# Attention: two query blocks of a stream multiplied with the values at once

## The chip, the cores and the metric

The kernel runs on 1 core of one Trainium2 chip. The metric is the device time of one execution in microseconds (us). Below, PE is TensorE (its matmuls), PEld its weight loads, ACT is ScalarE, DVE is VectorE, POOL is GpSimd, SP the engine whose queue issues the weight transfers.

## What is computed

Two layers of a transformer-like block over 256 latent tokens and 256 context tokens, all in float32. In each layer one input projection feeds an attention, two convolution branches and gates; then follow an output projection and a feed-forward part. The change is in the attention alone:

```
def attend(q_nope, q_rope, k_nope, k_rope, v):
    scale = (QK_NOPE + QK_ROPE) ** -0.5
    s = jnp.einsum('bqhd,bkhd->bhqk', q_nope, k_nope) + jnp.einsum('bqhr,bkr->bhqk', q_rope, k_rope)
    p = jax.nn.softmax(s.astype(jnp.float32) * scale, axis=-1).astype(v.dtype)
    return jnp.einsum('bqhk,bkhd->bqhd', p, v)
...
        att_c = attend(qc_nope, qc_rope, kc_nope, kc_rope, vc)
...
        att = blockwise_attend(q_nope, q_rope,
                               jnp.concatenate([k_nope, kc_nope], axis=1),
                               jnp.concatenate([k_rope, kc_rope], axis=1),
                               jnp.concatenate([v, vc], axis=1))
```

There are 8 heads, 64 value columns each. Latent queries see 512 keys (latent and context), context queries see 256 (context alone). The context stream is needed in layer 0 only.

## The kernel before

Every engine runs a program of its own, in an order that is written out by hand, and they meet at semaphores. The order of PE's work is that of the code of its block; no scheduler changes it.

The attention goes over four pairs of heads (pairs 0 to 3), and in a pair over the query blocks that `duos_of(l)` lists, 128 queries each: in layer 0 two latent blocks with four key tiles (`kt` = 4) and two context blocks with two (`kt` = 2), in layer 1 the two latent blocks. Block d of a pair goes through these steps, for both heads h of the pair:

- PE `scores(d, h)` (L2570): one product into the PSUM bank `scores` h, up to 512 columns wide.
- DVE `soften(d)`: the largest score (L1700); ACT `exps(d)`: the exponentials and their sum (L991); DVE: reciprocal (L1704) and the probabilities `PR` (L1706), which sets `prob_done`.
- PE `turn(d, h)` (L2579): `kt` transposes of 128 columns into the one PSUM bank `PT` ("probsT"); it waits for `prob_done` and for ACT's copy of the turn before it.
- ACT `copies(d)` (L1001): PSUM to SBUF, into `PTs`, one buffer for each head; it sets `turned_copied`.
- PE `attend(p, d)` (L2593): for each key tile and head one product, 64 weight columns (the values of a head) and 128 moving columns (turned probabilities of the block), accumulated in `attended` (`PV`). The two heads write to partitions 0 to 63 and 64 to 127. It waits for the copies of both heads, and sets `pv_done`.

In `pair(p)`, PE's order for each block but the last is: turn(d, 0), scores(d+1) for both heads, turn(d, 1), some other work, attend(d). The other work fills PE while ACT and DVE make the next block's probabilities: parts of a gate's projection (`gate_parts`, L2550 to L2552), or the next pair's keys and queries (`keys_tile`, `query_tile`, L2081 to L2083). For the last block it is turn(d, 0), gate work, turn(d, 1), gate work, attend(d), the rest of the gate. In the fp32 products the trace has two PE instructions for one of the program; the transposes have one.

ACT's order between two blocks matters too. After `copies(d)` and `exps(d+1)` it does, at one place of each pair, the gate's tanh (L966) and the rounding of a weight tile (`look`, L402), and before the last block's copies `keys_out` (L952, two instructions) and, for some pairs after the first of these copies, for others ahead of both, `queries_out` (L958, L960):

```
                    for d in range(len(duos) - 1):
                        copies(d)
                        exps(d + 1)
                        if d == NS[l] - 1:
                            gate_out(gate_a, p * 2)
                            look(next(looks))
                    if not last:
                        ...
                        keys_out(following[0])
                        if len(following) == 2:
                            copies(len(duos) - 1, [0])
                        queries_out(following[1])
```

`len(following) == 2` holds for pairs 0 and 2; pair 3 (`last`) has none of this.

Of the kernel before, what the change touches and what calls it, by code (L numbers as in the profile page):

```python
# [8 lines left out]
SEQ = 256  # L9
# [156 lines left out]
def build(nc, x, c, ctx_in, c_ctx, w_mod, b_mod, ln1_g, w_in, q_a_norm_g, w_q_b, kv_a_norm_g,  # L166
# [6 lines left out]
    with stack:  # L173
        def sb(name, shape, dt=F32):
            return stack.enter_context(nc.sbuf_tensor(name, shape, dt))
# [19 lines left out]
        ATT = sb("ATT", [P, 7 * T])  # L195
        Qb = ATT[:, 0:2 * T].rearrange("p (h n) -> p h n", h=2)
        Kb = ATT[:, 2 * T:4 * T].rearrange("p (h n) -> p h n", h=2)
        PTs = ATT[:, 4 * T:6 * T].rearrange("p (h n) -> p h n", h=2)
        ROW = ATT[:, 6 * T:7 * T]
        PR = sb("PR", [P, 2, T])  # L200
        KR = PR[NOPE:NOPE + ROPE, 0, :]
# [11 lines left out]
        RT = sb("RT", [P, 4])  # L213
        LINES = sb("LINES", [P, 2, D])
        GATE_ROW, GAIN_ROW = LINES[:, 0, :], LINES[:, 1, :]
        RSTD = sb("RSTD", [P, T])
        Z = sb("Z", [P, 2, T])
        TAB = sb("TAB", [P, 2, T])
# [212 lines left out]
        def duos_of(l):  # L431

            return [(s * SEQ + q * P, 2 * s, 4 - 2 * s) for s in range(NS[l]) for q in range(2)]
# [6 lines left out]
        def _(sp):  # L440
# [60 lines left out]
            for l in range(DEPTH):  # L501
# [51 lines left out]
                if l:  # L553
                    sp.dma_start(GAIN_ROW, final_g.partition_broadcast(P)).then_inc(rows_in, 16)
                if l == 0:
                    sp.wait_ge(pv_done, len(duos_of(0)) * PAIRS)
                sent = 0

                def loaded():
# [221 lines left out]
        def _(act):  # L781
# [101 lines left out]
            for l in range(DEPTH):  # L883
# [95 lines left out]
                def pair(p):  # L979

                    last, looks = p == PAIRS - 1, iter(pair_looks(p))
                    at.ring = 0

                    def exps(d):

                        kt = duos[d][2]
                        for h in range(2):
                            act.wait_ge(max_done, at.unit.n + (2 * d + h + 1))
                            if d:
                                act.wait_ge(turned, at.unit.n + (2 * d + h - 1))  # L990
                            act.activation(PR[:, h, 0:kt * P], S[h][:, 0:kt * P], ACT.Exp, bias=NM[:, h:h + 1],  # L991
                                           accum_out=RS[:, h:h + 1]).then_inc(exp_done, 1)

                    def copies(d, heads=range(2)):

                        kt = duos[d][2]
                        for h in heads:
                            act.wait_ge(turned, at.unit.n + (2 * d + h + 1))
                            if d:
                                act.wait_ge(pv_done, at.duo.n + d)  # L1000
                            act.activation(PTs[:, h, 0:kt * P], PT[:, 0:kt * P], ACT.Copy).then_inc(turned_copied, 1)  # L1001

                    exps(0)
                    look(next(looks))
                    gate_a = at.tile()
# [7 lines that stand above are left out]
                        following = [at.tile() for _ in range(3 if queries_kind(p + 1) == "fours" else 2)]  # L1013
# [4 lines that stand above are left out]
                    copies(len(duos) - 1, [1] if not last and len(following) == 2 else range(2))  # L1018
                    if not last:
                        look(next(looks))  # L1020
                        look(next(looks))
                    gate_b = at.tile()
                    act.wait_ge(pv_done, at.duo.n + len(duos))
                    act.activation(Uhi[:, p + AT0, 0:TQ], PV[:, 0:TQ], ACT.Copy).then_inc(op_hi, 1)
                    at.operand.next()
                    gate_out(gate_b, p * 2 + 1)
                    at.unit.n += 2 * len(duos)
                    at.duo.n += len(duos)

                for p in range(PAIRS):  # L1030
                    pair(p)
# [1022 lines left out]
        def _(pe):  # L2054
# [414 lines left out]
            for l in range(DEPTH):  # L2469
# [111 lines left out]

                def attend(p, d):

                    col, k0, kt = duos[d]
                    if d == 0 and p:
                        pe.wait_ge(op_lo, at.operand.n)
                    if d == 0 and p == 0:
                        for t in vt:
                            pe.wait_ge(drained[t.bank], t.drained)
                    pe.wait_ge(turned_copied, at.unit.n + 2 * d + 2)  # L2590
                    for k in range(kt):
                        for h in range(2):
                            last = pe.matmul(PV[h * VH:(h + 1) * VH, col:col + P],  # L2593
                                             V[:, k0 + k, (2 * p + h) * VH:(2 * p + h + 1) * VH],
                                             PTs[:, h, k * P:(k + 1) * P], start=k == 0, stop=k == kt - 1)
                    last.then_inc(pv_done, 1)

                for p in range(PAIRS):
# [11 lines left out]
                    for d in range(len(duos) - 1):  # L2610
# [8 lines left out]
                        else:  # L2619
# [5 lines left out]
                                nopes = query_tile(slot, 0)  # L2625
                            if fours and (d == 2 or l == 1):
                                query_tile(slot, 1)
                        attend(p, d)
                    d = len(duos) - 1
                    turn(d, 0)  # L2630
                    next(gate_b)
# [196 lines left out]
```

## Time and profile before

| | |
|---|---|
| time, median of 3 runs | 1222.69 us (1222.45 to 1223.12) |
| the profiled execution's own time | 1222.99 us |
| its span in the profile | 1221.2 us |
| busy: PE, DVE, ACT, POOL | 98%, 71%, 43%, 16% of the span |
| mean granted TensorE clock | 0.999 of full speed |

The attention of layer 0 lies at about 140 to 245 us of the span, that of layer 1 at about 864 to 928 us. A row of the timeline gives start, length, engine, line, operation, tiles, shapes, a count (several instructions of one kind are merged: the length then runs from the first one's start to the last one's end), and in brackets the engine's idle time before it with what ended it. PE's lengths overlap, since a matmul starts before the one ahead of it has left the array; what PE spends is therefore read from start to start.

### The profile page before, as it was taken

Reading aid. Unit: us, or ns where it says so; the run is one execution under the profiler, and the core shown is the slowest. Engines: PE = TensorE matmul, PEld = TensorE weight load, DVE = VectorE, ACT = ScalarE, POOL = GpSimd, SP = SyncE. Lnnn points to the kernel's source line nnn. Section 1 sums busy time; section 2 is a strip of 40 time slices with the busy share of each in tenths; the row PEclk is TensorE's granted clock in tenths of the full one; section 3 lists DMA queues with packets and bytes.
Section 4 is the critical chain, followed back from the end, with each engine's and each line's share of the span. In section 5 each row is a group of like instructions: output and inputs, shape, how many; then the busy total and the mean of one; then the engine's idle time right before and its main releaser. Section 6 shows DMA issues by size and latency. Waiting matters only on the chain.

```text
span 1221.2 us, 17807 instructions
## 1 busy us (share of the span) xinstructions
PE 1199.4 (98%) x6834; PEld 997.7 (82%) x6834; DVE 866.6 (71%) x1286; ACT 530.0 (43%) x891; POOL 191.9 (16%) x158
## 2 busy tenths in 40 slices
PE   7999999999999999999999999999999999999997
PEld 5777777788888898888888888889879999888886
DVE  4675766586887487678765666699887877766666
ACT  4342565522534352222222223465664555655554
POOL 0106993000001200000000000302980002000000
PEclk9999999999999999999999999999999999999999
DMA  9956322134464436557664665335434674666662
GB/s 296 315 153 206 84 54 69 36 86 132 110 178 131 156 105 191 152 163 217 187 193 153 209 192 157 101 90 149 122 114 113 168 212 138 201 196 190 181 198 87
DMA packets 265252, 188.88 MB, mean 155 GB/s; under 512 B 16035, under 2 KB 250833, under 8 KB 265169
## 3 DMA queue, kind: packets, MB, share of 16 engines
q1 hardware_dynamic: 264832, 187.60, 52.7%
q8 instruction: 55, 0.90, 0.3%
q14 instruction: 28, 0.23, 0.1%
q10 hardware_dynamic: 337, 0.15, 0.0%
HBM read 186.67 MB, written 1.05 MB: 154 GB/s over the span
## 4 chain that ended last, share of the span: by engine, by line
PE 89%; DVE 3%; ACT 3%; SPq 2%; issue 2%; DMA 1%; ACTq 0%; DVEq 0%
PE bank L2081 18%; PE bank L2083 17%; PE bank L2082 17%; PE bank L2122 5%; PE bank L2120 3%; PE scores L2570 3%; PE bank L2550 2%; PE bank L2552 2%; PE bank L2551 2%; PE probsT L2579 2%; PE attended L2593 1%; SPq L494 1%; ACT Whi L402 1%; DVE Wlo L413 1%; PE bank L2649 1%
## 5 line engine op out<-in xcount | busy, mean ns | idle before, releaser
L413 DVE TENSOR_TENSOR Wlo<-Wraw,Whi 128x1024 fp32r<-128x1024 f32 (+3 forms) x294 | 323.3, 1108 | 104.2 <-ACT Whi L402 103.1
L402 ACT ACTIVATE Whi<-Wraw 128x1024 fp32r<-128x1024 f32 (+1 forms) x296 | 270.4, 928 | 125.6 <-PE bank L2083 72.0
L2081 PE MATMUL bank<-Hhi,Whi 128*128 128x512 f32 (+1 forms) x786 | 285.6, 363 | 1.7 <-DVE Wlo L413 1.4
L2082 PE MATMUL bank<-Hlo,Whi 128*128 128x512 f32 (+1 forms) x786 | 281.6, 358 | 0.0
L2083 PE MATMUL bank<-Hhi,Wlo 128*128 128x512 f32 (+1 forms) x786 | 281.5, 358 | 0.0
L2081 PEld LDWEIGHTS bank<-Hhi,Whi 128*128 128x128 f32 x786 | 148.4, 189 | 30.6 <-issue 6.6
L2082 PEld LDWEIGHTS bank<-Hlo,Whi 128*128 128x128 f32 x786 | 148.5, 189 | 22.2 <-issue 1.0
L2083 PEld LDWEIGHTS bank<-Hhi,Wlo 128*128 128x128 f32 x786 | 148.5, 189 | 22.0
L2081 PE MATMUL bank<-Uhi,Whi 128*128 128x512 f32 (+1 forms) x350 | 128.3, 367 | 0.2 <-issue 0.2
L2083 PE MATMUL bank<-Uhi,Wlo 128*128 128x512 f32 (+1 forms) x350 | 126.5, 362 | 0.0
L2082 PE MATMUL bank<-Ulo,Whi 128*128 128x512 f32 (+1 forms) x350 | 126.5, 361 | 0.0
L670 POOL TENSOR_TENSOR SUM<-SUM,V 128x512 f32<-128x512 f32 (+1 forms) x21 | 28.4, 1354 | 486.9 <-ACT V L801 486.7
L2122 PE MATMUL bank<-Hhi,Whi 128*128 128x512 f32 x287 | 102.3, 396 | 0.0
L724 POOL TENSOR_SCALAR SUM<-U,PAR 128x512 f32<-128x512 f32 (+1 forms) x56 | 81.1, 1448 | 53.7 <-DVE ACC L1603 48.4
L2120 PE MATMUL bank<-Hhi,Wlo 128*128 128x256 f32 x328 | 84.7, 279 | 0.0
L2081 PEld LDWEIGHTS bank<-Uhi,Whi 128*128 128x128 f32 x350 | 66.0, 189 | 11.7 <-issue 2.1
L2083 PEld LDWEIGHTS bank<-Uhi,Wlo 128*128 128x128 f32 x350 | 66.0, 189 | 10.2
L2082 PEld LDWEIGHTS bank<-Ulo,Whi 128*128 128x128 f32 x350 | 66.1, 189 | 10.0 <-issue 0.2
L1848 DVE SCALAR_TENSOR_TENSOR X<-bank,MOD,X 128x256 f32<-128x256 f32 x64 | 28.1, 478 | 55.3 <-PE bank L2083 52.9
L791 ACT ACTIVATE V<-bank 128x512 f32<-128x512 f32 (+1 forms) x48 | 24.4, 508 | 94.7 <-PE bank L2083 94.7
L727 POOL TENSOR_TENSOR ACC<-ACC,SUM 128x512 f32<-128x512 f32 (+1 forms) x56 | 64.7, 1155 | 4.7
L1352 DVE SCALAR_TENSOR_TENSOR G<-ATT,CV,G 128x1024 f32<-128x1024 f32 x50 | 64.7, 1319 | 0.0
(309 smaller groups left out, 1977.6 us busy)
## 6 DMA issues: line engine op xcount, KB each, us to landing
Wraw<-in_w_ff SPq DMA_DIRECT2D x126, 512.0 KB, 3.9
Wraw<-in_w_in SPq DMA_DIRECT2D x78, 512.0 KB, 4.0
ATT<-in_w_mod SPq DMA_DIRECT2D x58, 512.0 KB, 4.5
Wraw<-in_w_o SPq DMA_DIRECT2D x16, 512.0 KB, 4.1
ACC<-in_w_mod SPq DMA_DIRECT2D x14, 512.0 KB, 4.4
Wraw<-in_w_mla_o SPq DMA_DIRECT2D x8, 512.0 KB, 3.5
ATT<-in_w_mod SPq DMA_DIRECT2D x12, 256.0 KB, 8.4
Wraw<-in_w_kv_b SPq DMA_DIRECT2D x12, 256.0 KB, 4.1
```

The costliest lines, as they stand in the source:

```text
L402: last = act.activation(hi, raw, ACT.Copy)
L413: last = eng.tensor_tensor(lo, raw, hi.bitcast(F32), ALU.subtract)
L670: pool.tensor_tensor(SUM[:, 0:n], SUM[:, 0:n], SQ[:, slot, 0:n], ALU.add).then_inc(sq_summed, 1)
L724: v = mark(pool.tensor_scalar(by_stream(SUM[:, :], l), U[:, 1, 0:NS[l], w:w + SEQ], PAR[:, l, CDW + 2 * w + 1:CDW + 2 * w + 2], None, ALU. ...
L727: ins = pool.tensor_tensor(by_stream(ACC[:, 1, :], l), by_stream(ACC[:, 1, :], l), by_stream(SUM[:, :], l), ALU.add)
L1352: last = dve.scalar_tensor_tensor(acc(s), raw, c, acc(s), mult, add)
L2081: pe.matmul(dst, sh, mh, start=j == 0, stop=False)
L2082: pe.matmul(dst, sh, ml, start=False, stop=False)
L2083: last = pe.matmul(dst, sl, mh, start=False, stop=j == k - 1)
L2120: last = pe.matmul(banks[t.bank][:, half[0]], Wlo[:, slot, w], Hhi[:, j, half[0]], start=False, stop=False)
L2122: last = pe.matmul(banks[t.bank][:, :], Whi[:, slot, w], Hhi[:, j, :], start=False, stop=j == DT - 1)
L2570: pe.matmul(S[h][:, 0:kt * P], Qb[0:NOPE + ROPE, h, col:col + P], Kb[0:NOPE + ROPE, h, k0 * P:(k0 + kt) * P], start=True, stop=True).then_ ...
```

## The change

`attend` is no longer called for every block but for every second one (odd d). It multiplies the turned probabilities of both blocks of a stream with the values at once: the same 64 weight columns, 256 moving columns. For this `PTs` holds both blocks: head 0's lie where both heads' buffers were (`ATT`), head 1's in `GATE_ROW` (`LINES`), which is used later, in layer 1, for something else. ACT's copy writes the `kt` tiles of 128 columns 256 columns apart instead of side by side. The waits on `pv_done` count half as many steps.

```
-        PTs = ATT[:, 4 * T:6 * T].rearrange("p (h n) -> p h n", h=2)
...
+        PTs = [w.rearrange("p (k n) -> p k n", k=4) for w in (ATT[:, 4 * T:6 * T], GATE_ROW)]
...
-                    sp.wait_ge(pv_done, len(duos_of(0)) * PAIRS)
+                    sp.wait_ge(pv_done, len(duos_of(0)) // 2 * PAIRS)
...
-                            if d:
-                                act.wait_ge(pv_done, at.duo.n + d)
-                            act.activation(PTs[:, h, 0:kt * P], PT[:, 0:kt * P], ACT.Copy).then_inc(turned_copied, 1)
+                            if d >= 2:
+                                act.wait_ge(pv_done, at.duo.n + d // 2)
+                            act.activation(PTs[h][:, 0:kt, d % 2 * P:(d % 2 + 1) * P],
+                                           PT[:, 0:kt * P].rearrange("p (k n) -> p k n", k=kt),
+                                           ACT.Copy).then_inc(turned_copied, 1)
...
-                    col, k0, kt = duos[d]
-                    if d == 0 and p:
+                    col, k0, kt = duos[d - 1]
+                    if d == 1 and p:
...
                     for k in range(kt):
                         for h in range(2):
-                            last = pe.matmul(PV[h * VH:(h + 1) * VH, col:col + P],
+                            last = pe.matmul(PV[h * VH:(h + 1) * VH, col:col + SEQ],
                                              V[:, k0 + k, (2 * p + h) * VH:(2 * p + h + 1) * VH],
-                                             PTs[:, h, k * P:(k + 1) * P], start=k == 0, stop=k == kt - 1)
+                                             PTs[h][:, k, :], start=k == 0, stop=k == kt - 1)
...
-                        attend(p, d)
+                        if d % 2:
+                            attend(p, d)
```

PE's order in layer 0, pair 0, from the end of the work that fills block 0 on, before (scores 128x256 are those of block 2; x8 counts the program's products):

```order
L2552 MATMUL bank<-Hhi,Wlo 128x512
L2593 MATMUL attended<-ATT,V 64x128 x8
L2579 MATMUL probsT<-IDN,PR 128x128 x4
L2570 MATMUL scores<-ATT 128x256 x2
L2579 MATMUL probsT<-IDN,PR 128x128 x4
L2081 MATMUL bank<-Uhi,Whi 128x512
L2082 MATMUL bank<-Ulo,Whi 128x512
L2083 MATMUL bank<-Uhi,Wlo 128x512
L2081 MATMUL bank<-Uhi,Whi 128x512
L2082 MATMUL bank<-Ulo,Whi 128x512
L2083 MATMUL bank<-Uhi,Wlo 128x512
L2593 MATMUL attended<-ATT,V 64x128 x8
```

The same place of the changed kernel, whose lines there are numbered two higher:

```order
L2554 MATMUL bank<-Hhi,Wlo 128x512
L2581 MATMUL probsT<-IDN,PR 128x128 x4
L2572 MATMUL scores<-ATT 128x256 x2
L2581 MATMUL probsT<-IDN,PR 128x128 x4
L2083 MATMUL bank<-Uhi,Whi 128x512
L2084 MATMUL bank<-Ulo,Whi 128x512
L2085 MATMUL bank<-Uhi,Wlo 128x512
L2083 MATMUL bank<-Uhi,Whi 128x512
L2084 MATMUL bank<-Ulo,Whi 128x512
L2085 MATMUL bank<-Uhi,Wlo 128x512
L2595 MATMUL attended<-ATT,V 64x256
L2595 MATMUL attended<-LINES,V 64x256
```

The eight products of block 0 are gone from between the filling work and turn(1, 0); after the next filling work stand eight of 256 columns (two are shown) in the place of eight of 128.

Layer 1, pair 0, from the end of the filling work to the place behind turn(1, 1), before:

```order
L2083 MATMUL bank<-Uhi,Wlo 128x256
L2593 MATMUL attended<-ATT,V 64x128 x8
L2579 MATMUL probsT<-IDN,PR 128x128 x4
L2550 MATMUL bank<-Hhi,Whi 128x256
L2551 MATMUL bank<-Hlo,Whi 128x256
L2552 MATMUL bank<-Hhi,Wlo 128x256
L2550 MATMUL bank<-Hhi,Whi 128x256
L2551 MATMUL bank<-Hlo,Whi 128x256
L2552 MATMUL bank<-Hhi,Wlo 128x256
L2579 MATMUL probsT<-IDN,PR 128x128 x4
L2550 MATMUL bank<-Hhi,Whi 128x256
L2551 MATMUL bank<-Hlo,Whi 128x256
```

And of the changed kernel:

```order
L2085 MATMUL bank<-Uhi,Wlo 128x256
L2581 MATMUL probsT<-IDN,PR 128x128 x4
L2552 MATMUL bank<-Hhi,Whi 128x256
L2553 MATMUL bank<-Hlo,Whi 128x256
L2554 MATMUL bank<-Hhi,Wlo 128x256
L2552 MATMUL bank<-Hhi,Whi 128x256
L2553 MATMUL bank<-Hlo,Whi 128x256
L2554 MATMUL bank<-Hhi,Wlo 128x256
L2581 MATMUL probsT<-IDN,PR 128x128 x4
L2552 MATMUL bank<-Hhi,Whi 128x256
L2553 MATMUL bank<-Hlo,Whi 128x256
L2554 MATMUL bank<-Hhi,Wlo 128x256
```

Here too the eight products ahead of turn(1, 0) are gone. The six products of the gate between turn(1, 0) and turn(1, 1) are the same, and what follows them ends in one `attend` of 256 columns. On ACT no instruction changes its place.

## Rows read from the trace of the kernel before

**Rows 1.** The profile page: part 1 (busy engines) and part 4 (the chain).

```profile
PE 1199.4 (98%) x6834; PEld 997.7 (82%) x6834; DVE 866.6 (71%) x1286; ACT 530.0 (43%) x891; POOL 191.9 (16%) x158
...
PE 89%; DVE 3%; ACT 3%; SPq 2%; issue 2%; DMA 1%; ACTq 0%; DVEq 0%
```

**Rows 2.** Groups of PE instructions by form: the products with the values.

```profile
L2593 PE MATMUL attended<-ATT,V 128*64 128x128 f32 x320 | 22.8, 280 | 0.0
```

**Rows 3.** Timeline of layer 0, pair 0, engine PE (start, length, line).

```profile
145.05 0.39 PE L2552 MATMUL bank<-Hhi,Wlo 128*128 128x512 f32 x1
145.28 0.60 PE L2579 MATMUL probsT<-IDN,PR 128*128 128x128 f32 x4
145.72 1.88 PE L2570 MATMUL scores<-ATT 96*128 96x512 f32 x4
...
150.41 0.39 PE L2552 MATMUL bank<-Hhi,Wlo 128*128 128x512 f32 x1
150.73 1.09 PE L2593 MATMUL attended<-ATT,V 128*64 128x128 f32 x16
...
152.24 1.03 PE L2570 MATMUL scores<-ATT 96*128 96x256 f32 x4
```

**Rows 4.** The same timeline at a query block with two key tiles.

```profile
159.36 0.39 PE L2083 MATMUL bank<-Uhi,Wlo 128*128 128x512 f32 x1
159.68 0.66 PE L2593 MATMUL attended<-ATT,V 128*64 128x128 f32 x8
```

**Rows 5.** Timeline of PE at 256-column products in column groups, outside the attention.

```profile
374.90 1.07 PE L2364 MATMUL scores<-ATT,ROWSEL 128*32 128x256 f32 x16
```

**Rows 6.** Timeline of DVE in layer 0, pair 0: normalised probabilities.

```profile
149.58 0.49 DVE L1706 TENSOR_SCALAR PR<-PR,RR 128x512 f32<-128x512 f32 x1
...
159.22 0.35 DVE L1706 TENSOR_SCALAR PR<-PR,RR 128x256 f32<-128x256 f32 x1
```

**Rows 7.** Timeline of PE in layer 1, pair 0.

```profile
875.06 0.66 PE L2579 MATMUL probsT<-IDN,PR 128*128 128x128 f32 x4
876.67 0.63 PE L2579 MATMUL probsT<-IDN,PR 128*128 128x128 f32 x4 [0.24 <-ACT ATT L1001]
```

**Rows 8.** Timeline of ACT and DVE in the same stretch.

```profile
871.67 0.60 ACT L1001 ACTIVATE ATT<-probsT 128x512 f32<-128x512 f32 x1 [1.56 <-PE probsT L2579]
...
873.76 1.07 ACT L402 ACTIVATE Whi<-Wraw 128x1024 fp32r<-128x1024 f32 x1
874.71 1.19 ACT L952 ACTIVATE ATT<-bank 64x512 f32<-64x512 f32 x2
875.92 0.60 ACT L1001 ACTIVATE ATT<-probsT 128x512 f32<-128x512 f32 x1
...
873.17 0.49 DVE L1706 TENSOR_SCALAR PR<-PR,RR 128x512 f32<-128x512 f32 x1
```

**Rows 9.** Timeline of ACT in layer 1, pairs 1 and 3.

```profile
892.60 0.38 ACT L960 ACTIVATE ATT<-bank 64x256 f32<-64x256 f32 x1
893.11 0.60 ACT L1001 ACTIVATE ATT<-probsT 128x512 f32<-128x512 f32 x1
...
923.47 1.07 ACT L402 ACTIVATE Whi<-Wraw 128x1024 fp32r<-128x1024 f32 x1
924.42 0.61 ACT L1001 ACTIVATE ATT<-probsT 128x512 f32<-128x512 f32 x1
```

**Rows 10.** Timeline of ACT and PE in layer 0, pair 1, last block.

```profile
189.03 0.60 ACT L960 ACTIVATE ATT<-bank 64x512 f32<-64x512 f32 x1
189.65 0.39 ACT L1001 ACTIVATE ATT<-probsT 128x256 f32<-128x256 f32 x1
...
190.23 0.39 PE L2579 MATMUL probsT<-IDN,PR 128*128 128x128 f32 x2
```

**Rows 11.** Timeline of PE and its loads in layer 0, pair 3.

```profile
238.02 0.41 PE L2579 MATMUL probsT<-IDN,PR 128*128 128x128 f32 x2 [0.36 <-ACT ATT L1001]
...
240.43 0.20 PEld L2579 LDWEIGHTS probsT<-IDN,PR 128*128 128x128 f32 x2 [0.26 <-DVE PR L1706]
```

More of the change, by code:

```diff
@@ L1022, in pair @@
                     gate_b = at.tile()
-                    act.wait_ge(pv_done, at.duo.n + len(duos))
+                    act.wait_ge(pv_done, at.duo.n + len(duos) // 2)
                     act.activation(Uhi[:, p + AT0, 0:TQ], PV[:, 0:TQ], ACT.Copy).then_inc(op_hi, 1)
@@ L1027, in pair @@
                     at.unit.n += 2 * len(duos)
-                    at.duo.n += len(duos)
+                    at.duo.n += len(duos) // 2
                 for p in range(PAIRS):
@@ L2582, in attend @@
                 def attend(p, d):
-                    col, k0, kt = duos[d]
-                    if d == 0 and p:
+                    col, k0, kt = duos[d - 1]
+                    if d == 1 and p:
                         pe.wait_ge(op_lo, at.operand.n)
-                    if d == 0 and p == 0:
+                    if d == 1 and p == 0:
                         for t in vt:
```

## The prediction

> **What bounds the kernel now.** I read the page first. PE is busy for 98% of the span and holds 89% of the chain that ended last, while DVE and ACT are far from full [rows 1]. So time is what PE spends from instruction to instruction, plus the few places where it waits. The second view is the groups of PE by form: the products with the values are 320 PE instructions (160 of the program) that keep PE busy for 22.8 us in all [rows 2], under 2% of the span. The change can only move some of that, and what stands around it. The third view is the timeline of PE, and there I read gaps from start to start. The fourth is the timeline of ACT and DVE at the same places, to see how long before PE's arrival a block's probabilities and copies were ready. That decides whether work taken away from PE makes it earlier or makes it wait.
>
> **The change part by part.** The number of weight loads and instructions is halved; the columns that stream are as many as before.
>
> One `attend` with four key tiles, in its place. With it, from the last product of the filling work to the scores behind the next turn, PE takes 152.24 - 150.41 = 1.83 us; at a place without one, the same stretch takes 145.72 - 145.05 = 0.67 us [rows 3]. So it costs 1.16 us. The 16 instructions last 1.09 us and the 8 of a block with two key tiles 0.66 us [rows 3, 4]: four steps, each with two instructions started together (one of each head), are 0.43 us, so a step is 0.108 us. The streaming of eight steps is then 0.86 us and the rest, 1.16 - 0.86 = 0.30 us, is paid once for each `attend`: going into products of 64 weight columns and out again. With two key tiles it is 1.16 - 0.43 = 0.73 us in its place.
>
> A step with 256 columns is not in the trace for these products. Bounds: below, twice 0.108 = 0.216 us. Above, (1.07 - 0.38) / 3 = 0.23 us from the 16 instructions of 256 columns that go in four column groups at once, four steps with the last instruction's 0.38 us taken off [rows 5]; that mean holds a longer first step, as every group has. I take 0.216. Widening an `attend` then adds 8 x 0.108 = +0.87 us with four key tiles and +0.43 with two. At 0.23 it would be +0.98 and +0.49, in all 0.9 + 0.2 = 1.1 us more.
>
> The Trainium skill, TensorEngine Tiling, section Tiling Modes, says that changing the tiling mode drains TensorE, while changing the tile within a mode doesn't. By that rule the 0.30 us are the two changes of mode around each `attend`, and the trace agrees with a loss of that kind; by that rule alone, each change of mode saved would be time saved, which is the first rival.
>
> Where the removed `attend` frees PE, PE goes straight on to turn(d+1, 0). Twelve are removed: eight in layer 0, four in layer 1. If nothing waits, each merge saves 1.16 - 0.87 or 0.73 - 0.43, both about -0.30 us. So each place has to be looked at.
>
> Layer 0, first merge of a pair (blocks 0 and 1), four times. Pair 0's probabilities of block 1 are ready at 149.58 + 0.49 = 150.07, and PE would come at 150.41 + 0.23 = 150.64 (0.23 us from a gate's last product to a turn, 145.05 to 145.28) [rows 3, 6]. 0.57 us to spare, and what follows (the copy, the turn of head 1) hangs on that turn alone. -0.29 each.
>
> Layer 0, second merge (blocks 2 and 3). In pairs 0 and 2 the probabilities of block 3 were ready at 159.22 + 0.35 = 159.57 and PE would have come at 159.36 + 0.23 = 159.59 [rows 4, 6]. That is no margin, but the work of ACT and DVE ahead of them moves 1.16 us earlier against PE, since it now falls beside the longer `attend` of block 1. -0.30 each, -0.59 a pair.
>
> Pair 1 is different: ACT does both instructions of `queries_out` ahead of the copy of turn(3, 0). It starts that copy at 189.65, right behind L960, and is done at 190.04; turn(3, 1) stood at 190.23 [rows 10]. With the usual 0.15 us from a copy's end to the turn behind it (875.92 + 0.60 to 876.67 [rows 7, 8]) it could come 0.04 us earlier and no more. The 0.73 us taken from PE there become a wait, and the widened `attend` adds 0.43. Pair 1: -0.29 - 0.04 + 0.43 = +0.10.
>
> Pair 3 has short filling work. PE waits 0.36 us for a copy at turn(2, 1) and then for the probabilities at turn(3, 0), 240.43 [rows 11]. The first wait goes away, since the longer `attend` of block 1 covers it; the second stays, but ACT's and DVE's chain up to it is 1.16 us earlier. So turn(3, 0) is 1.16 earlier, 0.06 more is saved behind it (a turn of four transposes lasts 0.66 us with an `attend` ahead of it and 0.60 without [rows 3, 7]), and +0.43 comes back: -0.79.
>
> Layer 0 in all: -0.59 - 0.59 + 0.10 - 0.79 = -1.87 us.
>
> Layer 1 is where the cost lies. In pair 0 ACT is busy without a gap from the copy at 871.67 on: copy, exponentials, gate, weight tile at 873.76, `keys_out` at 874.71, and only at 875.92 the copy of turn(1, 0), done at 876.52. Turn(1, 1) stands at 876.67 and had waited for it [rows 7, 8]. Turn(1, 0) itself at 875.06 could be 1.16 us earlier: its probabilities are ready at 873.17 + 0.49 = 873.66 [rows 8]. But turn(1, 1) can't, because nothing on ACT has moved. Thus the `attend` of block 0 lay in time in which PE would otherwise have waited. Taken away it gives nothing; put behind turn(1, 1), onto the path, it costs the whole +0.87 us. Pair 2 repeats this (no queries ahead of the copy). In pair 3 the copy at 924.42 follows the weight tile's start at 923.47 by 0.95 us [rows 9], the same 0.95 as from 873.76 to 874.71 [rows 8]: ACT is the limit there too. In pair 1 ACT ends `queries_out` at 892.60 + 0.38 = 892.98 and copies at 893.11 [rows 9], so 0.11 us can be had. Layer 1: 3 x 0.87 + 0.76 = +3.37 us.
>
> The same page of the skill, section Performance Considerations, warns that tiling speeds up TensorE but not the emptying of PSUM. Here the trace agrees in layer 1: the copy out of `probsT` is what turn(1, 1) waits for.
>
> The copies themselves: 48 of 0.60 or 0.39 us, now written 256 columns apart. The trace has no such write; the rows of copies from `probsT` side by side [rows 8, 10] are all there is. I take no change. Cover: in layer 1 there is none, three copies of a pair are on the path. No step is added on SP, POOL or DVE, and no transfer. SP's wait on `pv_done` ends at the same instruction of PE.
>
> Sum: -1.87 + 3.37 = +1.5 us. The profiled execution's own time is 1222.99, 0.3 above the median of 1222.69, and its span 1221.2. From 1222.99 it is 1224.5; against the median, **1224.2 us**.
>
> **The rivals.** (1) *Every merge pays.* Only the streaming and the 0.30 us of each `attend` count, and layer 1 doesn't wait for ACT. 12 x -0.29 = -3.5: 1219.2 us. It is decided by one thing: whether ACT can start the copy of turn(1, 0) in layer 1 as early as PE would then be done with it, 1.1 us ahead of 875.92. For: probabilities are ready in time nearly everywhere. Against: ACT's unbroken row up to 875.92 [rows 8]. This is where the Trainium skill's page TensorEngine Tiling, Tiling Modes, read alone, would lead.
>
> (2) *The spaced copy is slower.* Three copies a pair in layer 1 and one or two in layer 0 are on the path, some 18. From 0.06 us more for each, the kernel is slower by over 0.2%; at 0.1 it is +1.8: 1226.0.
>
> (3) *The two heads no longer run together at 256 columns.* A step becomes 0.43 us: 8 x 8 x 0.216 + 4 x 4 x 0.216 = +17 us, 1241. Against it: the 256-column products in column groups, 16 in 1.07 us [rows 5].
>
> (4) *The loss in layer 1 is partly absorbed*, by ACT reaching the copies sooner in two of the pairs: about 1222.7 to 1223.3.
>
> **How the numbers follow.** Forecast 0.65, its own range 1223.3 to 1225.6 (bounds of the step above, a few tenths for pairs 1 and 3). Rival 1 0.09, rival 2 0.12, rival 3 0.04, rival 4 0.10. 0.2% is 2.4 us, about what a measurement of this kernel can tell from no change: under 1220.3 is faster, over 1225.1 slower. Faster: 0.09. Slower: rivals 2 and 3, and the top of the forecast, 0.19. Same: 0.72. Range 1221.5 to 1226.1: it leaves out rival 1, rival 3 and the worse half of rival 2, about 0.18.
>
> **What would show it.** Right: `attended` in 160 PE instructions with starts in pairs 0.216 us apart; PE at turn(1, 0) of layer 1 1.1 us earlier than before within its pair and at turn(1, 1) not, with PE's wait for ACT's copy there grown from 0.24 [rows 7] to about 1.4 us in three pairs; the stretch of layer 1's attention 3.4 us longer, that of layer 0 1.9 shorter. Wrong: copies of L1001 longer than 0.60 and 0.39 us; a stretch of layer 1 that isn't longer; or a wait elsewhere, above all for DVE ahead of turn(3, 0) in layer 0.

## The result, and the profile after

The changed kernel takes **1226.45 us** (median of 11 runs, 1225.07 to 1227.15); the kernel before, run beside it 11 times, 1223.1. The ratio is **1.0026, 95% interval 1.0018 to 1.0034**: slower by 3.3 us, where 1.5 were forecast. The profiled execution took 1226.33 us, its span is 1224.4.

The page of the changed kernel (parts 1 and 4; before: [rows 1]):

```profile
PE 1197.0 (98%) x6674; PEld 993.8 (81%) x6674; DVE 867.4 (71%) x1286; ACT 531.2 (43%) x891; POOL 193.7 (16%) x158
...
PE 84%; DVE 4%; ACT 4%; DMA 2%; issue 2%; ACTq 0%; SPq 0%; DVEq 0%
```

PE has 160 instructions fewer and 2.4 us less busy time, and the kernel is slower. So the time lost is time in which PE waits: it isn't busy for 1224.4 - 1197.0 = 27.4 us, before 1221.2 - 1199.4 = 21.8. PE's share of the chain fell from 89% to 84%, which is far more than 3 us; it shows that the chain runs through waits for other engines more often, not how much they cost. The groups by form say that the operations themselves cost what was assumed (busy, mean ns; before: [rows 2, 8, 10]):

```profile
L2595 PE MATMUL attended<-LINES,V 128*64 128x256 f32 x80 | 19.8, 387 | 0.0
L2595 PE MATMUL attended<-ATT,V 128*64 128x256 f32 x80 | 19.7, 385 | 0.4
...
L1001 ACT ACTIVATE ATT<-probsT 128x512 f32<-128x512 f32 x16 | 9.6, 598 | 11.5 <-PE probsT L2581 11.4
```

The two halves of `attended` run beside each other, so 39.5 us of busy time are not 39.5 us of span. The copies that write 256 columns apart (head 0's are shown) take 598 ns, as long as those side by side (0.60 us in [rows 8]).

The timeline of the changed kernel, all that the text below reads (start, length, engine, line; in brackets the idle time before and what ended it):

```profile
140.62 0.59 PE L2572 MATMUL scores<-ATT 96*128 96x512 f32 x1
...
154.03 0.38 PE L2595 MATMUL attended<-ATT,V 128*64 128x256 f32 x1
...
155.33 0.38 PE L2595 MATMUL attended<-ATT,V 128*64 128x256 f32 x1
...
174.78 1.29 POOL L727 TENSOR_TENSOR ACC<-ACC,SUM 128x512 f32<-128x512 f32 x1
175.03 1.32 DVE L1708 TENSOR_SCALAR PR<-PR,RR 128x512 f32<-128x512 f32 x1
176.41 0.66 PE L2581 MATMUL probsT<-IDN,PR 128*128 128x128 f32 x4 [0.17 <-DVE PR L1708]
...
188.91 0.39 ACT L1001 ACTIVATE ATT<-probsT 128x256 f32<-128x256 f32 x1
189.44 0.41 PE L2581 MATMUL probsT<-IDN,PR 128*128 128x128 f32 x2 [0.53 <-ACT ATT L1001]
...
243.49 0.39 PE L2652 MATMUL bank<-Uhi,Whi 128*128 128x512 f32 x1
...
862.59 1.02 PE L2572 MATMUL scores<-ATT 96*128 96x512 f32 x2
...
872.26 0.60 PE L2581 MATMUL probsT<-IDN,PR 128*128 128x128 f32 x4
873.02 1.19 ACT L952 ACTIVATE ATT<-bank 64x512 f32<-64x512 f32 x2
874.23 0.60 ACT L1001 ACTIVATE ATT<-probsT 128x512 f32<-128x512 f32 x1
874.98 0.63 PE L2581 MATMUL probsT<-IDN,PR 128*128 128x128 f32 x4 [1.41 <-ACT ATT L1001]
875.64 0.60 ACT L1001 ACTIVATE LINES<-probsT 128x512 f32<-128x512 f32 x1
876.38 0.40 PE L2595 MATMUL attended<-ATT,V 128*64 128x256 f32 x1
...
929.47 0.39 PE L2652 MATMUL bank<-Uhi,Whi 128*128 128x256 f32 x1
...
1002.26 1.06 ACT L402 ACTIVATE Whi<-Wraw 128x1024 fp32r<-128x1024 f32 x1 [0.86 <-DMA Wraw<-in_w_o]
...
1004.64 0.39 PE L2312 MATMUL bank<-Uhi,Whi 128*128 128x256 f32 x1 [0.84 <-DVE Wlo L413]
```

The rows of the kernel before that answer to some of them and were not shown yet:

```profile
140.82 0.59 PE L2570 MATMUL scores<-ATT 96*128 96x512 f32 x1
...
174.96 1.30 POOL L727 TENSOR_TENSOR ACC<-ACC,SUM 128x512 f32<-128x512 f32 x1
175.83 0.71 DVE L1706 TENSOR_SCALAR PR<-PR,RR 128x512 f32<-128x512 f32 x1
...
245.19 0.39 PE L2649 MATMUL bank<-Uhi,Whi 128*128 128x512 f32 x1
...
864.28 1.02 PE L2570 MATMUL scores<-ATT 96*128 96x512 f32 x2
...
877.33 0.60 ACT L1001 ACTIVATE ATT<-probsT 128x512 f32<-128x512 f32 x1
877.98 1.09 PE L2593 MATMUL attended<-ATT,V 128*64 128x128 f32 x16
...
927.52 0.38 PE L2649 MATMUL bank<-Uhi,Whi 128*128 128x256 f32 x1
```

The first and the last product of a stage cut the span into pieces: the first scores of a layer's attention (L2572, before L2570) and the first output product behind it (L2652, before L2649). Layer 0 is 243.49 - 140.62 = 102.87 us, before 245.19 - 140.82 = 104.37; layer 1 is 66.88 us, before 63.24; behind it lie 1224.40 - 929.47 = 294.93 us, before 1221.21 - 927.52 = 293.69. So layer 0 gave 1.50 us, layer 1 cost 3.64, and **1.24 us were lost where nothing was changed**. With the start (-0.20) and the stretch between the layers (+0.01) that is the 3.19 us between the spans. All runs were cut in the same way. In the last two columns w_o is layer 1's first transfer of `in_w_o` behind the attention, and the load is explained at its experiment.

```
                          start   layer 0  (its pair 1)  layer 1   behind   load, us from first w_o issue
before                    140.8   104.37   28.32         63.24     293.69    +0.7
after                     140.6   102.87   28.77         66.88     294.93    +3.9
e1_again                  141.9   102.90   28.77         66.87     294.50    +3.8
e2_layer0_only            141.6   102.87   28.77         63.22     293.74    -3.3, +11.5
e3_layer1_only            140.7   104.50   28.36         66.88     293.75    -6.8,  +9.7
e4_moved_not_widened      140.5   103.00   28.82         66.96     293.75    +0.6
e5_early_waits            140.6   102.89   28.79         66.56     295.19    +3.7
e6_fewer_pool_taps        141.0   102.47   28.37         66.88     294.75    +3.6
e7_merged_copies_first    140.2   102.87   28.77         63.95     294.62    +4.0
e8_single_copies_first    140.6   104.49   28.35         64.21     293.74    +0.7
f1_load_moved_off         144.4   102.87   28.77         66.89     293.75    -1.8, +13.8
f2_load_moved_on          146.1   104.50   28.35         66.89     294.41    +3.6
f3_layer0_copy_first      140.4   102.17   28.06         63.22     293.75    -3.6, +11.9
f4_both_copies_and_waits  141.3   102.17   28.07         63.61     294.46    +3.6
```

The stages repeat within some 0.05 us from run to run, except the start, which moves by over a microsecond, and the stretch behind in the programs that are slow there. So one profile settles a few tenths of a stage, which the medians can't. For every program but f1 and f2, what the two layers and the stretch behind differ by adds up to within 0.5 us of the difference of the times (medians, where there are several executions).

### The profile page after: what moved, and what is told of

Read it like the earlier page. It is cut to its first block, busy times and chain, and to the rows that moved or that the text cites. A ratio compares the mean times of both kernels' runs of the same rounds, so it can differ in the third digit from the quotient of the medians.

```text
span 1224.4 us, 17471 instructions
## 1 busy us (share of the span) xinstructions
PE 1197.0 (98%) x6674; PEld 993.8 (81%) x6674; DVE 867.4 (71%) x1286; ACT 531.2 (43%) x891; POOL 193.7 (16%) x158
## 4 chain that ended last, share of the span: by engine, by line
PE 84%; DVE 4%; ACT 4%; DMA 2%; issue 2%; ACTq 0%; SPq 0%; DVEq 0%
PE bank L2083 17%; PE bank L2084 17%; PE bank L2085 16%; PE bank L2124 5%; PE bank L2122 3%; PE scores L2572 3%; PE bank L2552 2%; DMA Wraw<-in_w_in 2%; ACT Whi L402 2%; DVE Wlo L413 2%; PE bank L2554 2%; PE bank L2553 2%; PE attended L2595 1%; PE probsT L2581 1%; PE bank L2652 1%
## 5 line engine op out<-in xcount | busy, mean ns | idle before, releaser
L2085 PEld LDWEIGHTS bank<-Hhi,Wlo 128*128 128x128 f32 x786 | 148.5, 189 | 22.1
L724 POOL TENSOR_SCALAR SUM<-U,PAR 128x512 f32<-128x512 f32 (+1 forms) x56 | 84.6, 1510 | 53.7 <-DVE ACC L1605 48.4
L2085 PEld LDWEIGHTS bank<-Uhi,Wlo 128*128 128x128 f32 x350 | 66.0, 189 | 10.3
L2122 PEld LDWEIGHTS bank<-Hhi,Wlo 128*128 128x128 f32 x328 | 61.8, 188 | 3.5
```

The lines of the kernel that those rows point to most:

```text
L724: v = mark(pool.tensor_scalar(by_stream(SUM[:, :], l), U[:, 1, 0:NS[l], w:w + SEQ], PAR[:, l, CDW + 2 * w + 1:CDW + 2 * w + 2], None, ALU. ...
L2085: last = pe.matmul(dst, sl, mh, start=False, stop=j == k - 1)
L2122: last = pe.matmul(banks[t.bank][:, half[0]], Wlo[:, slot, w], Hhi[:, j, half[0]], start=False, stop=False)
```

## The experiments

**The changed kernel once more; each layer alone; the place without the width.** The products of a block are taken at their old place or both blocks' at the new one; `e4` has the new place and 128-column products, block d-1 and then block d. The buffers are the spaced ones in all of them. In this and the later cuts of code, conditions on a run's settings are written out.

```
+MODES = ['merged', 'single']     # e2; e3: ['single', 'merged']; e4: ['moved', 'moved']
...
+for b in {"single": [d], "moved": [d - 1, d], "merged": [d - 1]}[MODES[l]]:
+    col, k0, kt = duos[b]
+    c = slice(0, SEQ) if MODES[l] == "merged" else slice(b % 2 * P, (b % 2 + 1) * P)
...
-if d % 2:
+if d % 2 or MODES[l] == "single":
     attend(p, d)
```

> The changed kernel once more. In its first profile 2.15 us of the 3.3 lost lie in the two attentions (-1.5 in layer 0, +3.65 in layer 1) and 1.2 us behind them, in waits for weight transfers (0.2 us at about 980, 1.0 us at about 1004 us). Theory A: the part behind the attention is chance of one execution, so the two waits are not both there again and the difference to before is 2.0 to 2.6 us. Theory B: a later PE in layer 1 meets the transfers worse each time: both waits are there again and the difference is 3.2 to 3.6 us.

> Merged products in layer 0 alone; in layer 1 each query block has its products of 128 columns in their old place. Both theories: the attention of layer 0 is 1.5 us shorter and that of layer 1 as before (63.2 us from its first scores to the first product of the output), so 1221.6 us, 1.5 faster than before. If the spaced copies cost something, layer 1 is longer than before here too.

> Merged products in layer 1 alone. The attention of layer 1 is 3.6 us longer. Theory A: +3.6 us, 1226.7. Theory B: +4.8 us, 1227.9, with the waits for transfers behind the attention as in the changed kernel's first profile.

> The products of both blocks stay apart, 128 columns each, but stand together where the merged ones stand, in both layers. If the place alone decides, as I think, this is the changed kernel's time within 0.5 us (the same streaming, one entry into 64-column products saved just the same): 1225.3 to 1226.9. If the 256 columns themselves cost or save something (weight loads, the overlap of the two heads), it differs from the changed kernel by more, at 16 more loads for each pair.

Measured: e1 1225.58 us (ratio 1.0021, 1.0012 to 1.0031), e2 1221.08 (0.9986, 0.9977 to 0.9995), e3 1226.55 (1.0029, 1.0018 to 1.0040), e4 1225.21 (1.0018, 1.0009 to 1.0027). The stages add: layer 0 gives 1.5 us with layer 1 as it was, layer 1 loses 3.6 with layer 0 as it was. In e4 the attentions take 103.00 and 66.96 us, the changed kernel's within 0.13: **it is the place that costs and pays, not the width**. Sixteen 128-column products behind turn(1, 1) take what eight of 256 columns take there. The spaced copies alone cost 104.50 - 104.37 = 0.13 us in e3's layer 0 and nothing in e2's layer 1 (63.22 against 63.24). And e2, e3 and e4 lack the loss behind the attention that e1 has again. Neither theory of e1 holds as written. Its median is 2.55 us above the kernel before, as theory A has it, but the loss behind the attention isn't chance: it is back with 0.81 us. Of the two waits of theory B only the later one is back, 0.6 us instead of 0.8.

**Layer 1: the order of ScalarE.** In layer 1 the copies of the last block stand ahead of the next pair's `keys_out` and `queries_out`, as far as what they wait for allows; e7 with merged products, e8 with the products one block at a time.

```
+                        if l == 1 and len(following) == 2:
+                            copies(len(duos) - 1, [0])
                         keys_out(following[0])
+                        if l == 1:
+                            copies(len(duos) - 1, [1] if len(following) == 2 else range(2))
                         queries_out(following[1])
...
+                            if last and l == 1:
+                                copies(len(duos) - 1, [0])
                             look(next(looks))
```

> The changed kernel, and in layer 1 ACT copies the turned probabilities of block 1 before it copies keys and queries of the next pair (in pair 3 before it rounds a weight tile). If ACT's order is what makes the merge lose in layer 1, the merge now gets most of it back: pairs 0 to 2 are 0.85 us shorter, pair 3 0.35, the attention of layer 1 63.9 us instead of 66.9, and the whole about 1222.6 us (-2.9 against the changed kernel). If the wait was not ACT's order, at most 0.2 us a pair.

> The same order of ACT in layer 1, with the products of each block in their old place in both layers: what the order is worth without the merge. PE's turn(1, 0) bounds the copy there, so 0.17 us each in pairs 0 and 2, nothing in 1 and 3: layer 1 62.9 us, the whole 1222.6 us. If the order alone gave the 0.85 us of the merged one, it would be 1220.

Measured: e7 1223.43 us (ratio 1.0002, 0.9993 to 1.0011), layer 1 63.95 us: 2.93 less than in the changed kernel, within 0.05 us of what was expected. So ScalarE's order is the cause of 2.93 of the 3.64 us that layer 1 lost. The median was expected at 1222.6 and missed by 0.8, which is about the loss behind the attention. Timeline of e7, the same place as 872.07 to 876.38 above (lines some 5 to 22 higher):

```profile
871.79 0.60 PE L2599 MATMUL probsT<-IDN,PR 128*128 128x128 f32 x4
...
872.56 0.61 ACT L1006 ACTIVATE ATT<-probsT 128x512 f32<-128x512 f32 x1
873.03 1.20 ACT L957 ACTIVATE ATT<-bank 64x512 f32<-64x512 f32 x2
873.31 0.63 PE L2599 MATMUL probsT<-IDN,PR 128*128 128x128 f32 x4 [0.21 <-ACT ATT L1006]
...
874.99 0.40 PE L2617 MATMUL attended<-ATT,V 128*64 128x256 f32 x1 [0.35 <-ACT LINES L1006]
...
921.33 0.66 PE L2599 MATMUL probsT<-IDN,PR 128*128 128x128 f32 x4 [0.66 <-DVE PR L1726]
```

PE's wait of 1.41 us is down to 0.21. From turn(1, 0) to turn(1, 1) it is now 1.52 us, in the changed kernel 874.98 - 872.26 = 2.72. The last row is from pair 3, which is still 0.65 us longer than before the change: there PE comes to turn(1, 0) before DVE has the probabilities ready, and waits 0.66 us for them.

e8 missed: 1223.93 us (1.0010, 1.0001 to 1.0019), layer 1 64.21 us, 1.0 more than before and not 0.3 less. Its timeline shows why:

```profile
874.93 0.66 PE L2599 MATMUL probsT<-IDN,PR 128*128 128x128 f32 x4
...
875.62 0.60 ACT L1006 ACTIVATE ATT<-probsT 128x512 f32<-128x512 f32 x1 [0.93 <-PE probsT L2599]
876.12 1.19 ACT L957 ACTIVATE ATT<-bank 64x512 f32<-64x512 f32 x2
877.33 0.60 ACT L1006 ACTIVATE LINES<-probsT 128x512 f32<-128x512 f32 x1
...
877.98 0.32 PE L2617 MATMUL attended<-ATT,V 128*64 128x128 f32 x1 [0.27 <-ACT LINES L1006]
```

With the `attend` of block 0 ahead of turn(1, 0), PE reaches that turn late. ScalarE, which now has the copy next, stands idle for 0.93 us, does `keys_out` only then, and the second copy comes late behind it. The old order suits the old place of the products, the new order the new one; neither edit is good by itself.

**Layer 1: the waits that moved.** `op_lo` and the output banks' waits stand at block 0's place again, where before had them; the products stay merged. There is one execution.

```
+def ready(p):
+    if p:
+        pe.wait_ge(op_lo, at.operand.n)
+    else:
+        for t in vt:
+            pe.wait_ge(drained[t.bank], t.drained)
...
 if d % 2:
     attend(p, d)
+elif d == 0:
+    ready(p)
```

> The changed kernel, with the two waits that the first attend of a pair has besides the one for the copies (for the previous pair's output, or for the values) placed where block 0's attend stood before, ahead of turn(1, 0), instead of at the merged attend. In the changed kernel's trace the merged attend of layer 1 starts 0.14 us behind the end of the copy that it waits for, before it was 0.05. Theory: the second wait needs an instruction of its own behind the late one. Then each of the four pairs of layer 1 is 0.09 us shorter, 66.9 to 66.5 us in all. If the 0.09 us belong to the spaced copy or to the 256 columns, nothing changes.

Measured: layer 1 66.56 us, 0.32 less, 0.08 for each pair. In the changed kernel the first merged product starts 876.38 - 876.24 = 0.14 us behind the end of the copy that it waits for; before it was 877.98 - 877.93 = 0.05. That the second wait on the same instruction is what takes the time rests on this edit and its size; the wait has no row of its own in these views.

**Layer 0, pair 1: DVE beside GpSimd.** The kernel leaves out 20 of the 28 convolution taps that GpSimd computes in layer 0. There is one execution.

```
-for w in range(TAPS_BEFORE, TAPS):
+for w in list(range(TAPS_BEFORE, TAPS))[20 if l == 0 else 0:]:
```

> The changed kernel, without 20 of the 28 convolution taps that GpSimd computes in layer 0 (they are left out of the result), so that GpSimd is done before the attention. Theory: in pair 1 of layer 0 the probabilities of block 1 came late because DVE's multiplication took 1.32 us beside GpSimd's addition instead of 0.7. Then it takes about 0.5 us here, PE doesn't wait for it, and pair 1 is 0.3 us shorter, 28.77 to 28.4; the wait for ACT's copy at turn(3, 1) stays. If GpSimd is not the reason, pair 1 stays at 28.77.

Measured: pair 1 28.37 us instead of 28.77, the attention's other pairs as they were. DVE's row at the place of 175.03 above:

```profile
175.37 0.49 DVE L1712 TENSOR_SCALAR PR<-PR,RR 128x512 f32<-128x512 f32 x1
```

The same instruction takes 0.49 us with GpSimd idle, 0.71 in the kernel before and 1.32 in the changed one, where it starts 0.25 us behind the start of GpSimd's addition. In the kernel before it started 0.87 us behind it. In both it ends 0.28 us after that addition (176.35 against 176.07, and 176.54 against 176.26), so the 0.8 us by which DVE came earlier were lost again for the greater part.

**Layer 0, pair 1: the order of ScalarE.** Layer 1 as before, layer 0 merged, and there the copy of turn(3, 0) ahead of `queries_out` in pair 1 too. This is the version to which the experiments point.

```
+MODES = ['merged', 'single']
...
 keys_out(following[0])
-if len(following) == 2:
+if l == 0 or len(following) == 2:
     copies(len(duos) - 1, [0])
 queries_out(following[1])
...
+if l == 0:
+    copies(len(duos) - 1, range(2) if last else [1])
```

> Layer 1 as in the kernel before; layer 0 merged, and in its pair 1 ScalarE copies the last turned block ahead of the next queries' copies instead of behind them. If ScalarE's order is what holds the last turned block of pair 1 up: pair 1 falls from 28.8 us to 28.2 to 28.4, layer 0's attention from 102.9 to 102.3 to 102.5, the median to about 1220.6, ratio 0.998. If DVE beside GpSimd holds it up, or if the later queries' copies cost what the earlier copy gives, pair 1 stays at 28.7 to 28.8 and the median at 1221.1.

Measured: **1220.57 us, ratio 0.9981 (0.9972 to 0.9990)**, the fastest version here. Pair 1 takes 28.06 us, 0.71 less, which is more than was expected (28.2 to 28.4). Timeline of f3 at the place of 188.91 to 189.44 above, with the last instruction of `queries_out` (L965) now behind the copy:

```profile
187.50 0.39 ACT L1006 ACTIVATE ATT<-probsT 128x256 f32<-128x256 f32 x1
...
188.38 0.60 ACT L965 ACTIVATE ATT<-bank 64x512 f32<-64x512 f32 x1
188.58 0.38 PE L2599 MATMUL probsT<-IDN,PR 128*128 128x128 f32 x2
```

The wait of 0.53 us in front of turn(3, 1) is gone.

**Both orders and the waits together.** Both layers merged, with the edits of e7, f3 and e5.

> Both layers merged, the last turned blocks copied ahead of the next keys and queries in both layers, and TensorE's waits on V and on the output buffer put back to where the kernel before has them. If the two causes in layer 1 add (the order of ScalarE 2.9 us, the late wait 0.09 us a pair): layer 1's attention 63.6 us, layer 0's 102.4; the stretch behind stays at 294.6 to 295.2 as long as TensorE's instruction load meets the first w_o transfer; median 1222.4 to 1223.0. If the earlier copy has already hidden the late wait: layer 1 stays at 63.95 and the median at 1223.2.

Measured: 1222.0 us (ratio 0.9993, 0.9985 to 1.0002), layer 0 102.17, layer 1 63.61: the three causes add to within 0.05 us. The median is 0.4 us below the expected range, layer 0 0.2 shorter and the stretch behind 0.1 shorter than expected. Even so layer 1 is 0.37 us longer than before the change. Pairs 0 to 2 are 0.05 to 0.08 us shorter, pair 3 0.58 longer, as in e7.

**The stretch behind the attention.** The loss came with the changed program and not by chance: in every program with both layers merged, in none of e2, e3, e4 and e8. All layers' work there is the same instruction for instruction. What differs is how many instructions PE has done by then, and with it where the loads of its instructions fall. The queue q8 has 53 loads of 16 KB over the span in the changed kernel and 55 before, for 2 x 6674 and 2 x 6834 products and weight loads of PE: one for some 250 PE instructions each time, so these are PE's. For the table they were found by narrowing the window of the DMA view until one 16 KB packet was left in it. Seven runs have a load 3.6 to 4.0 us behind the first w_o issue, and those are the seven whose stretch takes 294.4 to 295.2 us; in the seven others it takes 293.69 to 293.75. The same seven also have a load 10.0 to 10.3 us ahead of that issue, which none of the others has, and in them the first w_o issue itself comes late: 64.2 to 64.5 us behind the first output product (994.0 - 929.47), in the others 63.9 (991.4 - 927.52). The DMA view of the changed kernel, 3 to 5 us behind that issue at 994.0:

```profile
q1 hardware_dynamic: 521, 0.26, 48.7%
q8 instruction: 1, 0.02, 5.8%
...
Wraw<-in_w_o SPq DMA_DIRECT2D x2, 512.0 KB, 5.8
```

And of the kernel before, 3 to 5 us behind its issue at 991.4:

```profile
q1 hardware_dynamic: 536, 0.27, 50.0%
...
Wraw<-in_w_o SPq DMA_DIRECT2D x2, 512.0 KB, 4.5
```

Two kernels move the loads without touching the attention or what follows. They move all loads together, and the start grows. Warm-up products at the very start are cut in two, which adds four PE instructions each: 27 of them in the changed kernel (f1), 15 in e3's kernel (f2). The expectations give the load's place as 0.7 to 1.2 us behind the issue; that was counted on the transfers' own zero, which is some 3 us off that of the timeline, and should read 3.6 to 4.0. For e3's kernel f2's expectation has 4.3, where the table has 9.7; its load moved by 6.1 us and not by the 3.4 asked for. That it still came to the place meant was luck; the table has the place where it fell.

```
 for _ in range(n):
-    pe.matmul(S[1][:, 0:P], ONES[:, :], ONES[:, :], start=True, stop=True)
+    halves = 2 if parted[0] else 1
+    parted[0] -= halves - 1
+    for c in range(halves):
+        w = P // halves
+        pe.matmul(S[1][:, c * w:(c + 1) * w], ONES[:, :], ONES[:, 0:w], start=True, stop=True)
```

> The changed kernel with its 27 warm-up products at the very start (128 columns each) cut into 54 of 64 columns: the same columns on TensorE, about 108 more instructions in its stream, and nothing else. TensorE's instructions are loaded in pieces of 256; in all five programs with both layers merged such a load (16 KB) came 0.7 to 1.2 us behind the issue of layer 1's first w_o transfer, and the stretch behind the attention was 0.8 to 1.5 us longer; in the five others it came elsewhere. Theory A (the place of this load costs the time): 108 instructions at some 0.055 us each move the load about 6 us ahead, so the stretch behind the attention falls from 294.5 to 295.2 us to 293.7, the wait of 0.8 us ahead of the gate product of the first w_o operand goes, the issues of the fourth and fifth w_o transfers take 0.37 us again instead of 0.8 to 1.6, and the median is 1.0 us below that of the changed kernel, less what the start may lose: 1224.9 to 1225.9. Theory B (the changed attention itself shifts the transfers against each other): the stretch stays at 294.5 or more and the median at 1225.6 to 1226.5. The attentions keep 102.9 and 66.9 us by both.

> The opposite of the run before: only layer 1 merged (there the stretch behind the attention was 293.75 us, and the load came 4.3 us behind the first w_o issue), with 15 of the warm-up products cut in two, 60 more instructions, which should bring the load to about 0.9 us behind that issue. Theory A: the stretch behind the attention becomes 294.5 to 295.2 us, with slow issues of the fourth and fifth w_o transfers, and the median goes from 1226.5 to about 1227.4. Theory B: it stays at 293.75 and the median at 1226.5.

Measured: with the load moved off, the stretch is 293.75 us although both layers are merged; with it moved on, 294.41 although only layer 1 is. Both go as theory A has it, in opposite directions (f2 0.1 us short of its range). So the place of the loads is the cause. Which of the two, the one 10 us ahead or the one 3.6 to 4.0 us behind, these two kernels can't tell apart, since both come and go together; what speaks for the second is that PE's main wait and the slow fourth and fifth issues lie behind it. The rows on the transfers, first of the changed kernel from 994.0 us on (issues' length in ns, min/median/max; who waited; time to landing):

```profile
L451 SPq DMA_DIRECT2D Wraw<-in_w_o x6: 368/379/1383, 994.0 to 1004.6; - x6
...
  PE bank L2312: 0.8, 1
...
DMA to landing us min/median/max: 4.0/5.7/6.2
```

of f1:

```profile
L455 SPq DMA_DIRECT2D Wraw<-in_w_o x6: 367/373/563, 997.1 to 1007.2; - x6
...
DMA to landing us min/median/max: 3.9/4.9/5.6
```

and of f2:

```profile
L455 SPq DMA_DIRECT2D Wraw<-in_w_o x6: 367/378/910, 1000.9 to 1011.1; - x6
...
  PE bank L2316: 0.4, 1
...
DMA to landing us min/median/max: 3.7/5.5/5.8
```

The issues grow from 0.37 to 1.38 and 0.91 us, the landings are 0.6 to 0.8 us later than in f1, and PE waits. The medians were missed: f1 1231.61 us (1.0077, 1.0059 to 1.0096) and f2 1232.95 (1.0082, 1.0068 to 1.0097). The cut warm-up is not free: 32 instructions of 64 columns last 7.06 us where 16 of 128 columns lasted 3.39, so a half takes the time of a whole. The start grew by 2.5 us (f1 against e1) and more, and f1's single times scatter from 1228.5 to 1237.6. So the medians say nothing on the load; the stage lengths do.

## Why the prediction was wrong

The direction, the mechanism of both layers and the sizes of the parts on PE were right. The time was 2.25 us too low, and the range missed by 0.35 us. By the prediction's own borders (over 1225.1 is slower) the result is "slower", which had 0.19, mostly for rivals 2 and 3, and these fell; "same" had 0.72. Part of the 2.25 isn't the change's: the forecast stood on 1222.69 for the kernel before, and beside the changed kernel that took 1223.1, 0.41 more; counted from there the range would just have held. The step that failed is the one that put everything outside the attention at nothing (1.24 us); two terms in the attention were too small (0.37 and 0.27 us). By its own steps:

- **A step of 0.216 us at 256 columns**: (155.33 - 154.03) / 6 = 0.217 us, over six steps. The upper bound of 0.23 wasn't needed. The third rival, the heads one after the other, fell.
- **-0.30 us for each merge where nothing waits**: pair 0 and pair 2 of layer 0 went from 26.25 us each to 25.66 and 25.64, -0.59 and -0.61; forecast -0.59. Pair 3: -0.74; forecast -0.79. That 0.30 us is paid once for each `attend` rests on e4 too, which saves as much with 128 columns. The Trainium skill, TensorEngine Tiling, Tiling Modes, says that a change of mode drains TensorE; what is saved in layer 0 agrees with it, and by that rule alone layer 1 would have gained as well.
- **Pair 1 of layer 0, +0.10**: it was +0.45. Here a step failed: "0.57 us to spare" was read in pair 0 and used for the first merge of all four pairs. In pair 1 GpSimd's additions run, DVE's normalisation took 1.32 us, and PE waited at turn(1, 0): the profile puts 0.17 us of idle time there, and without most of the taps the pair is 0.40 shorter. In that kernel (e6) pair 1 takes 28.37 us, +0.05, near the forecast. ScalarE's order was named as the limit of the second merge, rightly: undoing it gives 0.71 us (f3).
- **Layer 1, 0.87 and 0.76 for a pair**: measured +0.93, +0.84, +0.93, +0.94. That turn(1, 1) can't move was exact: PE waited 1.41 us there, forecast 1.4. The term left out is the 0.08 us a pair of the waits that moved with the first `attend` (e5) and that the step "The change part by part" gave no price. Without it layer 1 would be +3.32, forecast +3.37. The fourth rival, a loss partly absorbed, fell, and so did the first: it hung on ScalarE starting the copy early, which only an edit of its order brings (e7).
- **Spaced copies, no change**: 598 ns as before. Rival 2 fell.
- **Nothing outside the attention**: the sum put this at nothing, without looking where anything but the attention stood. "No step is added on SP, POOL or DVE, and no transfer" was true, and the sum ended there. Yet 160 products and 160 weight loads fewer moved the loads of PE's own instructions against the weight transfers, which cost 1.24 us in the profiled run, 0.8 in its repetition. It is the largest of the three errors (+0.37 and +0.27 are the other two). That it hits programs with both layers merged and spares those with one is a coincidence of counts: f1 is spared and f2 hit, and e4, with both layers moved but as many instructions as before, is spared.

Open is how the load does it, and which of the two loads. What the rows show is that one packet of 16 KB lies between six transfers of 512 KB, that SP's fourth and fifth issue take up to 1.4 us (1.6 in e5), and that the second w_o tile is late. A load 0.6 to 0.7 us behind the first issue (before, e4, e8) costs nothing. The profiled run of the changed kernel lost 0.4 us more there than its repetition: 0.2 at 980.50, where PE waits 0.28 us for DVE (in the repetition PE has no wait there), and 0.2 in the main wait, 0.84 against 0.61. Why they differ is open.

## What to carry to other kernels

Work on an engine may lie in time in which that engine would otherwise wait; taking it away there gives nothing, and putting it back behind the wait costs all of it. A merge of two steps should therefore be tried together with the order of the engine that feeds the second one, place by place: here layer 0 merged with the copy moved ahead gains 0.19%, layer 1 is best left alone. A margin read in one pair holds for that pair only, and each pair in which another engine is busy wants its own rows. And a change of some hundred instructions can shift the time in a stage that it doesn't touch by about 1 us, so that stage lengths, not medians, tell what an edit of this size does.

## What the runs showed of the hardware that was not expected

- PE's instruction loads (16 KB) cost time where they fall 3.6 to 4.0 us behind the first of six 512 KB transfers, with another load 10 us ahead of it: 0.7 to 1.5 us in seven profiled runs of seven, 0.0 to 0.1 in the seven others.
- DVE's scaling of 128x512 takes 0.49 us with GpSimd idle, and up to 1.32 us beside GpSimd's addition of the same size.
- At the start, an instruction of 64 columns with 128 weight columns took as long as one of 128: 7.06 / 32 = 0.22 us against 3.39 / 16 = 0.21. That the weight load is the limit there is a guess; it wasn't tried apart.
- A second wait in front of a product that also waits for a late copy cost 0.07 to 0.09 us in each of four pairs (e5, one execution); that the wait itself takes the time is argued from the edit.
